# Strided PSUM writes for gate building, and a new order for gates, rows and the last embedding blocks

## The reference

```
y = concat([y_mix, y_mem]) * silu(gate)
x = layer_norm(ALPHA * x + y @ w_out)
```

```
w = gelu(u[idx] @ h) * g          # g: softmax of the 16 best scores
x = x + sum(w * v[idx])
g_ple = sigmoid(rmsnorm(x) @ ple_gate)
x = x + g_ple * (p @ ple_proj)
```

## Time and profile before

| what | value |
|---|---|
| median of 3 runs | 3073.13 us (3072.13 to 3076.7) |
| profiled execution, its own time | 3074.83 us |
| its span, first to last instruction | 3072.7 us |
| mean granted PE clock | 0.966 |
| attention stage "b" with the gates | about 783 to 963 us |
| first pass, steps with quads | 2167 to 2430 us |
| second pass (`tile_sums`) | 2430 to 2938 us |
| last `row_add` | ends at 3028.15 us |

### The profile page before, as it was taken

The page is one execution under the profiler, slowest core; times in us unless marked ns, Lnnn a source line. Parts: engine busy times, 40 slices in busy tenths (PEclk is TensorE's granted clock), DMA queues, the critical chain, the costliest instruction groups (busy, mean ns, idle before and its releaser), DMA issues. The chain is left out here.

```text
span 3072.7 us, 28611 instructions
## 1 busy us (share of the span) xinstructions
PE 2788.7 (91%) x9498; PEld 1611.8 (52%) x9498; DVE 1863.5 (61%) x3615; ACT 776.8 (25%) x2034; POOL 733.1 (24%) x601
## 2 busy tenths in 40 slices
PE   9999999999888989998899988999988899988955
PEld 4454435454554444445655677878777544433422
DVE  4998622008774232347742667999667777657784
ACT  1114310102331011344531231212444311112122
POOL 0530000000000000002210355444100255545672
PEclk9999999999999989999999999999999999999977
DMA  5221112212001221110022599998544599999993
GB/s 192 78 86 55 69 73 91 82 55 82 29 28 41 82 85 56 58 55 28 28 89 94 207 382 378 343 320 319 209 131 132 188 409 409 409 412 390 398 375 138
DMA packets 125763, 544.44 MB, mean 177 GB/s; under 512 B 13888, under 2 KB 14272, under 8 KB 117568
## 3 DMA queue, kind: packets, MB, share of 16 engines
q0 software_dynamic: 73728, 268.47, 23.1%
q1 hardware_dynamic: 49472, 258.02, 22.5%
q10 hardware_dynamic: 2432, 16.29, 1.4%
HBM read 538.52 MB, written 4.19 MB: 177 GB/s over the span
## 5 line engine op out<-in xcount | busy, mean ns | idle before, releaser
L1142 PE MATMUL ps<-XTD,STREAM 128*128 128x256 f32 x2048 | 461.6, 384 | 21.9 <-ACT GD L1641 13.5
L1170 PE MATMUL ps<-STREAM,GD 128*128 128x512 f32 x1024 | 458.3, 604 | 23.0 <-DMA STREAM<-experts 17.8
L606 PE MATMUL ps<-XT,W 128*128 128x512 f32 (+1 forms) x1216 | 471.8, 548 | 6.9 <-issue 4.5
L1142 PEld LDWEIGHTS ps<-XTD,STREAM 128*128 128x128 f32 x2048 | 387.5, 192 | 82.3 <-DMA STREAM<-experts 16.5
L1801 POOL DMA_INDIRECT ROW_U<-peer_u,C x208 | 254.4, 1223 | 470.2 <-DVE DOT L2448 444.6
L606 PEld LDWEIGHTS ps<-XT,W 128*128 128x128 f32 x1216 | 229.6, 190 | 248.0 <-issue 238.4
L1170 PEld LDWEIGHTS ps<-STREAM,GD 128*128 128x128 f32 x1024 | 190.7, 192 | 288.7 <-issue 207.6
L2460 DVE SCALAR_TENSOR_TENSOR X<-ROW_V,WEIGHT,X 128x1024 f32<-128x1024 f32 x208 | 267.1, 1284 | 98.6 <-DMA ROW_V<-peer_v,C 82.3
L2448 DVE CUSTOM_DVE_ANT_0 ROW_U<-ROW_U,XN 128x1024 f32<-128x1024 f32 x208 | 253.8, 1220 | 62.9 <-DMA ROW_U<-peer_u,C 55.5
L1810 POOL DMA_INDIRECT ROW_V<-peer_v,C x208 | 234.2, 1126 | 155.6 <-DVE X L2460 119.1
L721 PE MATMUL ps<-W,Y 128*128 128x512 f32 x512 | 225.5, 601 | 13.1 <-DVE Y L1972 6.1
(11 more groups left out here) (347 smaller groups left out, 3827.8 us busy)
## 6 DMA issues: line engine op xcount, KB each, us to landing
STREAM<-experts SPq DMA_DIRECT2D x256, 512.0 KB
W<-wstream SPq DMA_DIRECT2D x53, 2048.0 KB, 8.4
GD<-wstream ACTq DMA_DIRECT2D x2, 2048.0 KB, 15.7
ROW_U<-peer_u,C POOLq DMA_INDIRECT x208
ROW_V<-peer_v,C POOLq DMA_INDIRECT x208
XT<-xT SPq DMA_DIRECT2D x8, 256.0 KB, 5.3
W<-wstream SPq DMA_DIRECT2D x8, 256.0 KB, 5.8
X<-x SPq DMA_DIRECT2D x1, 2048.0 KB, 19.5
```

What stands on the lines that cost most here:

```text
L606: mm = pe.matmul(b[:, 0:rhs[k].shape[-1]], w[:, k, m * P:(m + 1) * P], rhs[k], start=(k == 0), stop=(k == KD - 1))
L1142: mm = pe.matmul(UP_BANK[g % 2][:, 0:256], u[:, k, :], XTD[:, k, :], start=(k == 0), stop=(k == KD - 1))
L1170: mm = pe.matmul(acc(b, n)[:, :], GD[:, i * 256 + b * P:i * 256 + (b + 1) * P], STREAM[m % STREAM_RING][:, n * T:(n + 1) * T], start=(i == ...
```

## The change

The quad products are written with a step of four elements in PSUM, so that a bank holds tile by tile four tokens, and `DENSE`, the view of `GD`, is walked in the same order (tile outside, four neighbouring tokens inside). `ones_ahead` lets DVE and ACT make the one-hot rows of a next quad before they finish the quads of this step, and rows now stand ahead of `quad_gates`. `rows_by` counts one row for two steps after g = 82 instead of one for four. The attention gate uses tanh: silu(x) = x * (1 + tanh(x/2)) / 2, with one DVE operation, and the half inside the product with the head's output. At the end PLE index 1 and 2 (blocks 2, 3) are interleaved, use other PSUM banks, and the projection of index 3 stands ahead of its transposes.

```diff
+def ones_ahead(g):
+    free = quads_by(g - 1) + 2
+    return [q for q in quads_of(g + 1) if q < free], [q for q in quads_of(g + 1) if q >= free]
 def rows_by(g):
...
-    return rows_by(QUAD_FROM) + (g - QUAD_FROM) // 4
+    return rows_by(QUAD_FROM) + (g - QUAD_FROM) // 2
+def routed_by_row(r):
+    first, due = rows_by(TILES - 1), UNITS // 2 * UNIT_ROWS - 4
+    steps = ROUTE_STEPS + 1
+    return 12 * ROUTE_STEPS + 6 + (steps * (r - first + 1) // (due - first) if r < due
+                                   else steps + steps * (r - due + 1) // UNIT_ROWS)
-        DENSE = GD[:, :].rearrange("p (i t) -> p t i", i=TILES)
+        DENSE = GD[:, :].rearrange("p (i t) -> p i t", i=TILES)
-        PLE_T = ((2, 3), (2, 3), (2, 3), (4, 5))
-        PLE_S = ((0, 1), (0, 1), (0, 1), (6, 7))
+        PLE_T = ((2, 3), (2, 3), (4, 5), (2, 3))
+        PLE_S = ((0, 1), (0, 1), (6, 7), (0, 1))
+        PLE_J = ((2, 3), (2, 3), (4, 5), (6, 7))
@@ build_quad
-                    mm = pe.matmul(BUILD_BANK[q % 3][:, i * P:(i + 1) * P], ONE[q % 2][:, 1, i, :], ONE[q % 2][:, 0, i, :],
+                    mm = pe.matmul(BUILD_BANK[q % 3][:, :].rearrange("p (i t) -> p t i", t=4)[:, i, :], ONE[q % 2][:, 1, i, :],
@@ PE, end
-                if i in (100, 101):
-                    ple_gates(0, i - 100)
-                if i == 103:
+                if i in (102, 103):
+                    ple_gates(0, i - 102)
+                if i == 105:
                     ple_proj(0)
-            for i in range(1, 4):
-                ple_transposes(i)
+            ple_transposes(1)
+            ple_transposes(2)
+            for i in (1, 2):
                 ple_gates(i, 0)
                 ple_gates(i, 1)
                 ple_proj(i)
+            ple_proj(3)
+            ple_transposes(3)
+            ple_gates(3, 0)
+            ple_gates(3, 1)
@@ ACT, gate of the attention; step g of the first pass; end
-                act.activation(gate_tile("b", j), FILL_BANK[j % 2][:, :], ACT.Exp, scale=-1.0).then_inc(gate_exp, 1)
+                act.activation(gate_tile("b", j), FILL_BANK[j % 2][:, :], ACT.Tanh, scale=0.5).then_inc(gate_half, 1)
+                ahead, behind = ones_ahead(g)
+                for q in ahead:
+                    scale_quad(q)
+                row_weights(rows_by(g) - LAG)
                 for q in quads_of(g):
                     keep_quad(q, g)
-                for q in quads_of(g + 1):
+                for q in behind:
                     scale_quad(q)
-                row_weights(rows_by(g) - LAG)
-            for i in (2, 3):
-                ple_copies(i)
-                ple_roots(i)
-                ple_sigmoid(i)
+            ple_sigmoid(2)
+            ple_copies(3)
+            ple_roots(3)
+            ple_sigmoid(3)
@@ DVE, the same places
-                dve.tensor_scalar(g, g, 1.0, None, ALU.add).then_inc(gate_part, 1)
-                dve.wait_ge(gate_part, 2 * j + 1)
-                dve.reciprocal(g, g).then_inc(gate_part, 1)
-                dve.wait_ge(gate_part, 2 * j + 2)
-                dve.tensor_tensor(g, g, FILL_BANK[j % 2][:, :], ALU.mult).then_inc(gate_done, 1)
+                dve.scalar_tensor_tensor(g, g, 1.0, FILL_BANK[j % 2][:, :], ALU.add, ALU.mult).then_inc(gate_done, 1)
+                ahead, behind = ones_ahead(g)
+                for q in ahead:
+                    quad_ones(q)
                 if gated(g) > 0:
                     tile_gates(g)
+                rows_to(rows_by(g))
                 for q in quads_of(g):
                     quad_gates(q, g)
-                for q in quads_of(g + 1):
+                for q in behind:
                     quad_ones(q)
-                rows_to(rows_by(g))
-                if r == ROWS - 20:
+                if r == ROWS - 17:
                     add_sums(2)
                     add_sums(3)
-                if r == ROWS - 14:
+                if r == ROWS - 16:
                     ple_scale(1)
-                if r == ROWS - 10:
+                if r == ROWS - 15:
+                    ple_scale(2)
...
-            for i in (2, 3):
-                ple_scale(i)
-                ple_factor(i)
-            for i in (2, 3):
-                ple_out(i)
+            ple_out(2)
+            ple_scale(3)
+            ple_factor(3)
+            ple_out(3)
```

More of the change, by code:

```diff
@@ L1159, in build_quad @@
                 for i in range(4):
-                    mm = pe.matmul(BUILD_BANK[q % 3][:, i * P:(i + 1) * P], ONE[q % 2][:, 1, i, :], ONE[q % 2][:, 0, i, :],
-                                   start=True, stop=True)
+                    mm = pe.matmul(BUILD_BANK[q % 3][:, :].rearrange("p (i t) -> p t i", t=4)[:, i, :], ONE[q % 2][:, 1, i, :],
+                                   ONE[q % 2][:, 0, i, :], start=True, stop=True)
                 mm.then_inc(built, 1)
@@ L1204, in ple_proj @@
                 pe.wait_ge(loaded_proj, 32)
+                if i == 3:
+                    pe.wait_ge(ple_gate_ready, 6)
                 for n in range(2):
                     for k in range(2):
-                        mm = pe.matmul(ps[PLE_T[i][n]][:, :], PLE_P[:, k, b * P:(b + 1) * P], w[:, k, n * T:(n + 1) * T],
+                        mm = pe.matmul(ps[PLE_J[i][n]][:, :], PLE_P[:, k, b * P:(b + 1) * P], w[:, k, n * T:(n + 1) * T],
                                        start=(k == 0), stop=(k == 1))
@@ L1296, in att_steps @@
                         if t == gate_step(stage, j) + 1:
-                            (gate_silu if stage == "a" else gate_exponential)(j)
+                            (gate_silu if stage == "a" else gate_tanh)(j)
             def out_projection(name, n, roots=1):
@@ L1654, in keep_quad @@
                 act.wait_ge(built, q + 1)
-                act.activation(DENSE[:, 4 * q:4 * q + 4, g + 1:TILES],
-                               BUILD_BANK[q % 3][:, :].rearrange("p (t i) -> p t i", t=4)[:, :, g + 1:TILES], ACT.Copy
+                act.activation(DENSE[:, g + 1:TILES, 4 * q:4 * q + 4],
+                               BUILD_BANK[q % 3][:, :].rearrange("p (i t) -> p i t", t=4)[:, g + 1:TILES, :], ACT.Copy
                                ).then_inc(gates_kept, 1)
@@ L1954, in att_steps @@
                             dve.wait_ge(bank_free, POS["gate_b"] + head + 1 + 4)
-                        dve.tensor_tensor(yt(y), OT_BANK[head % 2][:, :], gt(y), ALU.mult).then_inc(at_y, 1)
+                        if stage == "b" and head >= 4:
+                            dve.scalar_tensor_tensor(yt(y), OT_BANK[head % 2][:, :], 0.5, gt(y), ALU.mult, ALU.mult
+                                                     ).then_inc(at_y, 1)
+                        else:
+                            dve.tensor_tensor(yt(y), OT_BANK[head % 2][:, :], gt(y), ALU.mult).then_inc(at_y, 1)
             att_steps("a")
@@ L2472, in rows_to @@
                     r = done_rows
-                    while routed < UNITS and 32 * routed - r <= 10:
+                    while routed < UNITS and 32 * routed - r <= 4:
                         draw_to(drawn + 1)
@@ L2549, in ple_out @@
                     dve.wait_ge(ple_proj_full, 2 * i + n + 1)
-                    ch.link(dve.tensor_tensor(gate, gate, ps[PLE_T[i][n]][:, :], ALU.mult))
+                    ch.link(dve.tensor_tensor(gate, gate, ps[PLE_J[i][n]][:, :], ALU.mult))
                     dve.tensor_tensor(xb(b)[:, cols], xb(b)[:, cols], gate, ALU.add).then_inc(y_ready, 1)
```

40 lines of the change are left out of this document (23 added, 17 removed).

## The result

The changed kernel takes 2965.23 us, the median of 4 runs (2960.07 to 2974.43). The kernel before, run beside it, takes 3073.68 (3072.13 to 3076.7). The ratio is 0.9649, with an interval of 0.9624 to 0.9674: 108 us faster.

What follows compares the result with a forecast made beforehand. It saw four places with different limits: PE's waits in attention and quad steps, DMA (then DVE) in the second pass, PE in the tail. 21 + 9 + 28 + 19 = 77 us gained; forecast 2996 us, range 2972 to 3040.

Steps and rivals of the forecast that it cites:

- the sum's first term: Attention stage: the tanh gate removes PE's listed wait for ACT's copy, 21 us gained, bounds 10 to 26.
- Rival 3: Attention stage: most of the wait stays, as the copy waits in a pipeline of several engines; 3014 us, 6%.
- the second term: Quad steps: 21 us of PE waiting against 31 before, so 9 us gained; bounds all 31 to a loss of 19.
- 11 x 1.4: Quad steps: on 11 row steps with two quads, PE waits 1.4 us each.
- 11 x 0.5: Quad steps: on 11 row steps with one quad, PE waits about 0.5 us each.
- What gates cost: Quad steps: with four tokens side by side, `quad_gates` falls from 1089 ns to about 625.
- Strided products: Quad steps: build matmuls writing PSUM with a step cost 0 us more; 41 us kept as the alternative.
- rivals 1 and 5: Quad steps: strided products cost twice their columns (3037 us, 18%) or four times the column time (3119 us, 3%).
- Rows: Second pass and rows left over: 11 more rows done early save 28 us, bounds 12 to 34.
- Rival 4: Quad steps: the 11 rows cost there what they save later, or gates stay at 2.13 ns; 3024 us, 9%.
- Rival 2: Quad steps: all waits vanish, as DVE has free time and one-hot rows are ahead; 2974 us, 10%.
- Tail: Last row to the end: 25 us instead of 44.5, so 19 us gained, bounds 12 and 22.

Runs made afterwards that it cites:

- e1: The kernel before with only the tanh gate of the attention added: 3043.93 us, ratio 0.9893.
- e2: The kernel before with only the strided products and the new walk of `DENSE`: 3049.49 us, ratio 0.9906.
- e3: The changed kernel with contiguous products and the old walk of `DENSE` put back: 2995.31 us, ratio 0.9734.
- e4: The changed kernel with one row for four steps in the quad steps, 11 rows instead of 22: 2983.15 us, ratio 0.9692.
- e6: The changed kernel with no one-hot rows made ahead, rows still in front of the gates: 2992.48 us, ratio 0.9732.
- e7: The changed kernel with products written contiguously and read by ACT and DVE with a step in PSUM, new walk kept: 2962.23 us, ratio 0.9639.
- e5: The changed kernel with the old end, its PSUM banks and engine order as before: 2985.69 us, ratio 0.9703.

## Why the prediction was wrong in size and mostly right in its mechanisms

**Attention gates: the sum's first term was too small, 21 against 35.** The step that failed is "Only PE's wait was on the path: 20.5 us. What is late next is PE itself, whose other 159 us are matmuls". Two things were on the path beside it. PE also waited for DVE's products with the gates at the end of the stage, 4.7 us before and 1.2 after, which I had left out. And between waits PE's matmuls are not at their pace: the same 722 took 161.0 us of busy time with the waits and 153.0 without, at a clock of 0.97 and 1.00. That makes 20.5 + 3.5 + 8.0 = 32.0 us in the stage, and 3.1 more behind it. My upper bound of 26 allowed 5 us for the clock, which is about the 4.6 that it cost, and nothing for the rest. e1 gives the sizes alone: 32.0 and 3.4. The stage now takes 154.8 us, of which PE is busy for 153.0, so PE is indeed the limit, as forecast. Rival 3 fell.

**Quad steps: the second term was too small, 9 against 27.** The waits after were well forecast in sum, 21 us against 18.1 in the list, and in part for the right reason. Behind an even step with a row and two quads PE waited ten times, 1.44 us on average, where I had 11 x 1.4. The 11 x 0.5 did not come; in their place stand five waits of 0.7 to 0.8 us ahead of a second quad. What failed is what the sum was compared with: "11 x 1.4 + 11 x 0.5 = 21 us of waiting against 31 before". The 31 were the listed idle time, and the pace of PE was taken from the length of a burst ("beside 3.62 us of tile products"). By the spacing of starts the steps before lost 48.4 us, not 31, and 48.4 - 23.6 = 24.8 of the 26.8 us follow; the other 2.0 are the last step, 7.0 us before and 5.0 after.

The 48.4 us can be taken apart. 30.7 are 43 listed waits. The listed idle counts only from where the last matmul of a burst has drained, so each of them was 0.16 us longer than listed, 7.0 in all: the wait of 0.52 us was in truth 0.68. 3.1 are 18 second builds that came 0.17 us late and list 0.01 us or so. 6.1 are 61 late starts whose second matmul came 0.10 us late as well. 1.6 is one stretch of 3.4 us at 1.2 GHz. e2, e3, e4 and e6 repeat it: their lost time (20.2, 56.0, 11.0, 50.4) orders their stage lengths (233.8, 269.7, 223.8, 263.1), and what is left of each is 212.7 to 213.7 us, against 212.6 in the changed kernel and 214.6 before.

**What gates cost: right.** Forecast about 0.6 us, measured 0.586 (e7: the same). The Trainium skill's rule for lines of 16 bytes ("SBUF — State Buffer", Door 1) fits: runs of four fp32 in place of single ones took `quad_gates` from 1089 to 586 ns.

**Strided products: right at 0.** Eight take 1.16 us with and without a step. The sentence of the Trainium skill that any non-contiguous pattern slows matmuls significantly ("PSUM — Partial Sum Buffer", Specifications (TRN2)) does not hold for these fp32 products with a step of 16 bytes; rivals 1 and 5 fell with it. My reason for the 0, two cycles for a column, was argued and not tested. The working beside it was off by the same burst lengths: 226 and 145 ns for 256 and 128 columns are 216 and 112 from start to start, so 128 columns more cost 104 ns, not 81, and only 8 ns of the smaller matmul are not columns.

**Rows: right, 28 against 27.1.** The second pass with its remainder got shorter by 27.1 us, and e4 shows that the 11 rows are worth 26, by the second of my two workings: they would stand behind the pass at 2.5 us each. What I did not foresee is how the 27 divide. The pass took 494.9 us and not the 507 that I named. The 12 us do not come from the early rows, since e4, with its rows late, has them too, and there the rows left over take 12 us longer than before in exchange. They are lost at PLE index 0, where PE stood 11.17 us before and no longer stands; the change moved that work and also spread the routing steps, and no run separates the two.

**The cost of the added rows.** I had them at up to 2.55 us each; e4 gives 12.4 / 11 = 1.1. Rival 4 fell. Rival 2, 2974 us by the loss of all waits, came nearest in time, but for another reason, since 18.1 us of waits remain; it had 10%.

**Tail: right, 19 against 19.3.** 25.3 us from the last sum to the end were forecast as 25. The projection of PLE index 3 (block 1) stood 9.7 us for the sigmoid that frees its bank, which was the reason for my bound of 12, but it did so ahead of the last row, where it costs nothing. e5 undoes the term alone: 20 us, 19.0 of them behind the last row.

**The range** was built from bounds that shared one flaw: in the two terms that missed, the most that could be won was the listed idle time, in the attention with 5 us for the clock. Both misses went to the same side for the same reason.

## What to carry to other kernels

What an engine can win back is its stage length less its number of instructions times their spacing from start to start in an unhindered stretch, not the sum of its listed waits: here the list showed 24.0 of 32.0 us in one stage, of which I had counted 20.5, and 31 of 48 in another. When a DVE or ACT operation scatters single fp32 over SBUF, turn the walk round so that four neighbours lie side by side; on which side of PSUM the step then stands made no difference. Work that is pulled forward into a chain should come with something made ahead there: the eleven rows cost 1.1 us each with the one-hot rows ahead, and without them the whole gain of the stage was gone.

## What was unexpected of the hardware

- Matmuls into PSUM with a step of four fp32 run at the pace of contiguous ones: 112 ns start to start for one of the eight of 128 columns (e7 against the changed kernel).
- DVE and ACT read PSUM with a step of 128 elements as fast as contiguously: 586 ns and 239 ns, against 586 and 238.
- Waits cost PE more than the idle time: the same 722 matmuls were busy for 161.0 us with waits and 153.0 without. 4.6 of the 8.0 us are three stretches at 1.2 GHz; at the others the second matmul of 128 columns after a wait started 0.21 us behind the first, not 0.11.
- The second pass keeps 397 to 405 GB/s with 11 rows more or less to come, and its own length does not change by them (493.6 us in e4, 494.9 in the changed kernel); the bytes of 11 rows fit into the quad steps, where the engines went from 137 to 202 GB/s.
- A reciprocal takes 3353 ns for 512 elements and 1.75 us for 256, so 6.3 ns for each further element, but half of one for each gate cost PE only 0.31 us.
